# A two-block transformer step on one core: the two-sided matmul form also for the last merge gates and five output projections, and matmuls of one width in runs of eight

## What is computed

```python
u = jnp.einsum('bsd,de->bse', xn, w_in[l])
q, k, v, xr, gr, ga, gb = jnp.split(u, splits, axis=-1)
ya = chunked_band_attention(q, k, v, rel_table[l]) @ w_attn_out[l]
yb = (hr * jax.nn.gelu(gr)) @ w_rnn_out[l]
gates = jax.nn.sigmoid(jnp.concatenate([ga, gb], axis=-1) + b_merge[l])
h = h + (g_a * ya + g_b * yb) @ w_o[l]
gu = hn @ w_ffn_in[l]
h = h + (jax.nn.silu(g) * up) @ w_ffn_out[l]
...
    h = h + mix.astype(h.dtype)
    h = h + squared_relu_mlp(rmsnorm_2(h, mlp_norm_g[i]), mlp_w_up[i], mlp_w_down[i])
```

## Time and profile before

| | |
|---|---|
| median of 3 runs | 1126.56 us (1125.75 to 1126.63) |
| the profiled execution | 1126.75 us, its span 1125.0 us |
| PE busy, matmuls recorded | 1112.1 us (99%), 7954 |
| DVE, ACT, POOL busy | 765.5, 589.9, 218.3 us |
| mean granted clock of PE | 0.998 |

### The profile page before, as it was taken

One profiled execution on the slowest core, in us unless ns is written; L12 is line 12 of the kernel. 1 busy time (PEld: TensorE's weight loads), 2 busy tenths in 40 slices (PEclk: granted clock), 3 DMA queues, 4 the chain that ended last, 5 costly groups with the idle time before them and its releaser, 6 DMA issues.

```text
span 1125.0 us, 19980 instructions
## 1 busy us (share of the span) xinstructions
PE 1112.1 (99%) x7954; PEld 1037.1 (92%) x7954; DVE 765.5 (68%) x943; ACT 589.9 (52%) x791; POOL 218.3 (19%) x216
## 2 busy tenths in 40 slices
PE   8999999999999999999999999999999999999997
PEld 8999999999888889999999988888899999888887
DVE  6656985666877754699886777764467657876443
ACT  6547557535655543665664556643354445665332
POOL 2995003302000000167844010000030002000000
PEclk9999999999999999999999999999999999999999
DMA  9774442655655555446410356555545444655541
GB/s 296 214 229 150 150 140 93 224 181 175 200 186 186 186 192 188 145 149 188 150 39 2 112 164 197 195 192 186 187 150 188 151 145 148 198 191 214 188 149 38
DMA packets 154994, 187.31 MB, mean 166 GB/s; under 512 B 6544, under 2 KB 143920, under 8 KB 154928
## 3 DMA queue, kind: packets, MB, share of 16 engines
q1 hardware_dynamic: 151360, 184.06, 50.2%
q10 hardware_dynamic: 3568, 2.31, 0.7%
HBM read 185.29 MB, written 1.07 MB: 166 GB/s over the span
## 4 chain that ended last, share of the span: by engine, by line
PE 87%; POOL 5%; DVE 5%; issue 1%; ACT 1%; DMA 0%; DVEq 0%; SPq 0%; POOLq 0%; ACTq 0%
PE PS L445 18%; PE PS L492 12%; PE PS L386 10%; PE PS L387 9%; PE PS L388 9%; PE PS L447 9%; PE PS L494 6%; POOL XN L910 2%; DVE WL L382 2%; POOL XN L905 1%; POOL TAP L908 1%; PE PS L453 1%; PE PS L452 1%; PE PS L454 1%; PE PS L2012 1%; PE PS L2025 1%
## 5 line engine op out<-in xcount | busy, mean ns | idle before, releaser
L382 DVE TENSOR_TENSOR WL<-RAW,WH 128x2048 fp32r<-128x2048 f32 x170 | 399.5, 2352 | 213.1 <-ACT WH L373 213.0
L373 ACT ACTIVATE WH<-RAW 128x2048 fp32r<-128x2048 f32 x170 | 325.0, 1912 | 219.1 <-PE PS L494 121.1
L445 PE MATMUL PS<-XHL,WH 128*128 128x512 f32 x864 | 300.9, 395 | 0.0
L386 PE MATMUL PS<-XHL,WH 128*128 128x256 f32 x832 | 239.9, 288 | 3.6 <-DVE WL L333 2.4
L447 PE MATMUL PS<-XHL,WL 128*128 128x256 f32 x864 | 239.7, 277 | 0.0
L388 PE MATMUL PS<-XHL,WL 128*128 128x256 f32 x832 | 235.4, 283 | 0.0
L387 PE MATMUL PS<-XHL,WH 128*128 128x256 f32 x832 | 235.4, 283 | 0.0
L492 PE MATMUL PS<-HHL,WH 128*128 (+1 forms) x592 | 205.4, 394 | 0.0
L445 PEld LDWEIGHTS PS<-XHL,WH 128*128 128x128 f32 x864 | 162.1, 188 | 37.5
L386 PEld LDWEIGHTS PS<-XHL,WH 128*128 128x128 f32 x832 | 159.5, 192 | 7.2 <-issue 2.8
L494 PE MATMUL PS<-HHL,WL 128*128 (+1 forms) x592 | 164.0, 277 | 0.0
(11 more groups left out here) (310 smaller groups left out, 1669.7 us busy)
## 6 DMA issues: line engine op xcount, KB each, us to landing
RAW<-in_mlp_w_up SPq DMA_DIRECT2D x32, 1024.0 KB, 5.4
RAW<-in_mlp_w_down SPq DMA_DIRECT2D x32, 1024.0 KB, 5.0
RAW<-in_w_in SPq DMA_DIRECT2D x25, 1024.0 KB, 5.2
RAW<-in_w_ffn_in_pairs SPq DMA_DIRECT2D x22, 1024.0 KB, 5.1
RAW<-in_dn_w_in SPq DMA_DIRECT2D x16, 1024.0 KB, 5.8
RAW<-in_mb_w_in SPq DMA_DIRECT2D x12, 1024.0 KB, 5.1
RAW<-in_w_ffn_out SPq DMA_DIRECT2D x11, 1024.0 KB, 4.9
RAW<-in_w_attn_out SPq DMA_DIRECT2D x4, 1024.0 KB, 5.7
```

Of the source, the lines that this page charges most:

```text
L373: act.activation(WH[:, k], RAW[:, k], ACT.Copy).then_inc(hi_done, 1)
L382: dve.tensor_tensor(WL[:, k], RAW[:, k], WH[:, k].bitcast(F32), ALU.subtract).then_inc(lo_done, 1)
L386: pe.matmul(out, wh, xh, start=start, stop=False, skip_group_check=True)
L445: pe.matmul(out, h[:, k, part], XHL[:, k].rearrange("p e t -> p (e t)"), start=(k == 0), stop=False, skip_group_check=True)
```

## The change

The wide form is also used for the last four chunks of gab, for ao, ro (but its last chunk), wo, do and mo. `OH` and `OL` become halves of one tensor `OHL`, `DOH` and `DOL` of `DOHL`, so that 512 columns can be read in one matmul. A table `PAIRS` names the two banks of each such chunk. In every wide chunk the order of the matmuls changes: the 512-column ones of a block (or, in `multiply_rows`, of a k) come first, then its 256-column ones; in chunks in pieces, and where `multiply_rows` goes by b, in twos.

In gab, ao and ro ACT copies the second half to SBUF (`low_to`) and DVE adds the first (`add_to`), then multiplies as before. In wo, do and mo DVE adds both halves to `H`, one after the other. The last chunk of ro stays narrow (`halves_=False`) in the first half of its banks. The gate of the eighth chunk moves behind its copy.

```diff
+        PAIRS = {"qk": (4, 6, 2, 4, 6, 2, 4, 6), "gab": (None, None, None, None, 3, 5, 0, 3), "ao": (5, 0, 2, 4),
+                 "ro": (6, 0, 4, 2), "wo": (6, 4, 2, 6), "do": (6, 4, 2, 6), "mo": (5, 2, 0, 6)}
...
-            for n, (b, k) in enumerate(order_of(pieces)):
...
+            runs = [[(b, k) for k in range(KB)] for b in range(2)]
+            if pieces is not None:
+                runs = [[(b, k) for k in (p, p + 1)] for p in range(0, KB, 2) for b in range(2)]
+            for n, run in enumerate(runs):
...
-                pe.matmul(out, h[:, k, part], XHL[:, k].rearrange("p e t -> p (e t)"), start=(k == 0), stop=False,
-                          skip_group_check=True)
-                mm = pe.matmul(out[:, TOK:512], l[:, k, part], XH[:, k], start=False, stop=(k == KB - 1),
-                               skip_group_check=True)
+                for _, k in run:
+                    pe.matmul(out, h[:, k, part], both[:, k].rearrange("p e t -> p (e t)"), start=(k == 0), stop=False,
+                              skip_group_check=True)
+                for _, k in run:
+                    mm = pe.matmul(out[:, TOK:512], l[:, k, part], both[:, k, 0], start=False, stop=(k == KB - 1),
+                                   skip_group_check=True)
...
+            runs = [[(k, b) for b in range(KB)] for k in range(KROWS)]
+            if narrow or first or left == 3:
+                runs = [[(k, b) for k in range(KROWS)] for b in range(KB)]
...
+        def low_to(act, st, out):
+
+            act.wait_ge(mm_done, st.count())
+            act.activation(out, wide_sides(st)[1], ACT.Copy).then_inc(s_.part_out, 1)
+
+        def add_to(dve, st, out, n):
+
+            dve.wait_ge(s_.part_out, n)
+            return dve.tensor_tensor(out, out, wide_sides(st)[0], ALU.add)
...
                 merge_gate(2 * st.j - 8)
-                merge_gate(2 * st.j - 7)
+                if st.j < 7:
+                    merge_gate(2 * st.j - 7)
+                act.wait_ge(s_.scanned, 8)
+                low_to(act, st, GAB[:, 2 * st.j:2 * st.j + 2])
+            merge_gate(7)
...
                     dve.wait_ge(mm_done, st.count())
-                    dve.tensor_tensor(hb, hb, bank(st), ALU.add).then_inc(freed[st.slot], 1)
+                    ch(dve.tensor_tensor(hb, hb, wide_sides(st)[1], ALU.add))
+                    ch.wait(dve)
+                    dve.tensor_tensor(hb, hb, wide_sides(st)[0], ALU.add).then_inc(freed[st.slot], 1)
...
-            steps(pe, seg["ao"], lambda st: multiply(pe, st, OH, OL))
-            steps(pe, seg["ro"], lambda st: multiply(pe, st, XH, XL, (s_.y_done, 0) if st.j == 0 else None))
-            steps(pe, seg["wo"], lambda st: multiply(pe, st, OH, OL, (s_.ml_done, 0) if st.j == 0 else None))
+            steps(pe, seg["ao"], lambda st: multiply_wide(pe, st, both=OHL))
+            steps(pe, seg["ro"], lambda st: multiply_wide(pe, st, (s_.y_done, 0) if st.j == 0 else None, halves_=st.j < 3))
+            steps(pe, seg["wo"], lambda st: multiply_wide(pe, st, (s_.ml_done, 0) if st.j == 0 else None, both=OHL))
```

More of the change, by code:

```diff
@@ L430, in wide_sides, with multiply_wide @@
             return both[:, :, 0], both[:, :, 1]
-        def multiply_wide(pe, st, pieces=None, between=None):
+        def multiply_wide(pe, st, pieces=None, between=None, both=XHL, beside=None, halves_=True):
             pe.wait_ge(lo_done, st.count())
@@ L475, in multiply_rows @@
             first = st.i is None and st.j == 0
[L476 to L485, removed]
+            narrow = left in (1, 2)
@@ L486, in multiply_rows, with operands @@
+            def operands(k):
+                xhl = HHL[:, bass.ds(st.rel * KROWS + k, 1)].rearrange("p k e t -> p (k e t)")
+                return xhl, xhl[:, 0:TOK], xhl[:, TOK:512]
+            runs = [[(k, b) for b in range(KB)] for k in range(KROWS)]
+            if narrow or first or left == 3:
+                runs = [[(k, b) for k in range(KROWS)] for b in range(KB)]
+            for run in runs:
+                b = run[0][1]
+                if first and b % 2 == 0:
                     wide_bank_read(pe, wide, (2, 2, 6, 4)[b // 2])
-                if left == 2 and k == 0 and b % 2 == 0:
+                if left == 2 and b % 2 == 0:
@@ L488, in multiply_rows @@
                     pe.wait_ge(s_.low_added, 4 * (row_no[st.seg.name] - 1) + b // 2 + 1)
[L489 to L495, removed]
@@ L496, in multiply_rows @@
-                if left == 3 and b % 2 and k == KROWS - 1 and b < KB - 1:
+                for k, b in run:
+                    part = slice(b * P, b * P + P)
+                    xhl, xh, xl = operands(k)
+                    if narrow:
+                        mm = product(pe, PS[:, ROW_BANK[b], 0:TOK], h[:, k, part], l[:, k, part], xh, xl, False,
+                                     left == 1 and k == KROWS - 1)
+                    else:
+                        pe.matmul(PS[:, ROW_BANK[b]], h[:, k, part], xhl, start=first and k == 0, stop=False, skip_group_check=True)
@@ L497, in multiply_rows @@
+                for k, b in [] if narrow else run:
+                    mm = pe.matmul(PS[:, ROW_BANK[b], TOK:512], l[:, k, b * P:b * P + P], operands(k)[1], start=False,
+                                   stop=left == 3 and k == KROWS - 1, skip_group_check=True)
+                if left == 3 and b % 2 and b < KB - 1:
                     mm.then_inc(s_.low_rows, 1)
-                if left == 1 and b < KB - 1 and k == KROWS - 1 and (b % 2 or st.seg.name == "w1" and b == KB - 2):
+                if left == 1 and b < KB - 1 and (b % 2 or st.seg.name == "w1" and b == KB - 2):
@@ L1539, in _ @@
                     mix_lo(st.j - 1)
[L1540 to L1541 removed]
+                if st.j < 3:
+                    ch(add_to(dve, st, MU[:, blk], part_no("ro") + st.j + 1))
+                    ch.wait(dve)
+                    sum_ = MU[:, blk]
+                else:
+                    dve.wait_ge(mm_done, st.count())
+                    sum_ = wide_sides(st)[0]
+                dve.tensor_tensor(MU[:, blk], sum_, GAB[:, 8 + 2 * st.j:10 + 2 * st.j], ALU.mult).then_inc(freed[st.slot], 1)
                 dve.wait_ge(freed[st.slot], st.base // SLOTS + 1)
@@ L2150, in _ @@
             attn_pv(pe, 11)
-            steps(pe, seg["mo"], lambda st: multiply(pe, st, OH, OL, None if st.j else (s_.ol_done, 8)))
+            steps(pe, seg["mo"], lambda st: multiply_wide(pe, st, None if st.j else (s_.ol_done, 8), both=OHL))
             mlp(1)
```

48 lines of the change are left out of this document (33 added, 15 removed).

## The result

The changed kernel takes 1128.4 us (median of 17 runs, 1127.8 to 1129.3) where the kernel before takes 1126.5 beside it (17 runs, 1125.4 to 1127.0). The ratio is 1.0019, with a 95% interval of 1.0012 to 1.0026. The change makes the kernel slower by about 2 us; 1123.3 was forecast. The profiled execution of the changed kernel took 1128.9 us, its span 1127.2, against 1126.75 and 1125.0 before.

A forecast was written before the change was run, and what follows sets the result against it. PE, busy 99%, was taken as the bound: number of matmuls times their spacing. Terms -5.0 + 0.5 + 1.0 + 0.1 = -3.4 us, with 0 for the order, gave 1123.3 us; range 1102 to 1132.

The forecast's parts named there:

- The products that become wide: In 23 chunks of gates, attention and recurrence outputs, wo, do and mo, 368 products save 0.0137 us each: -5.0 us.
- The runs: Wide chunks in eights or twos: the new order moves no total, 0 us, with bounds of -18.9 and +8.3 us.
- reading by starts: Wide chunks in runs: 512 columns keep 0.2315 us, 256 pay 0.120; +8.3 us, 1131.5 us; chance 0.17.
- The cheaper runs: Wide chunks: a 512-column matmul behind its own kind falls to about 0.2155 us; 1104.6 us in all; chance 0.29.
- the skill's rule: Warm matmuls follow at N/2.4 + 2.5 ns, so 1824 wide products take 40 us less; kept as a rival.
- The gate wait: At the fifth gate chunk ACT's copy delays the eighth chunk's weight split, so PE waits: +0.5 us.
- The norm waits: After the last chunk of wo, do and mo, DVE's second addition makes PE wait 0.3 us, three times: +1.0 us.
- do: First do chunk: the saving in its first two pieces is lost, the third piece starting at about 628: +0.1 us.
- The slow start that goes: Before the norm sums 24 pairs take 0.354 us each instead of 0.347; whether that goes does not count.
- a pattern of its own: A long run of 512-column matmuls could have its own spacing pattern; named as a way to be wrong, without size.

The follow-up runs named there:

- experiment 5: Changed kernel with six blocks of 48 extra matmuls of various column and weight widths, onto a bank nothing reads, in one u0 chunk; 1174.5 us, single execution.
- experiment 2: Kernel before with only the matmul order changed, to runs of eight, in the chunks already wide; projections still narrow; 1129.5 us, ratio 1.0028.
- experiment 3: Changed kernel with runs of sixteen where possible, both blocks' 512-column matmuls before their 256-column ones; 1126.5 us, ratio 0.9999 to the kernel before.
- experiment 4: Changed kernel with runs of four instead of eight; 1131.3 us, ratio 1.0044 to the kernel before.
- experiment 1: Changed kernel with wide chunks in the old alternating order (512, 256, 512, 256) instead of runs; 1127.8 us, ratio 1.0012 to the kernel before.
- experiment 6: Changed kernel in alternating order, with the last chunk of wo, do and mo narrow; 1124.5 us, ratio 0.9985 to the kernel before.
- run 120: Not a follow-up run: "run" is a verb here, and 120 is the ns between starts of 256-column matmuls, 213 in some profiled executions.

## Why the prediction was wrong

**The products that become wide: right.** 368 matmuls fewer, and the projections gain. From the terms with the measured runs and waits one gets -5.0 + 0.9 (the runs in their own 23 chunks) + 0.5 + 1.6 + 0.1 - 0.5 (loose pairs that are gone, see below) = -2.4 us, against -2.3 in the three segments that hold nearly all of them.

**The runs: wrong, and this is the step that failed.** "Runs of either kind would move no total", so the term was 0. They moved it by +4.4 us, which turns -3.4 into +1.0. The prices of a settled matmul were read rightly, and experiment 5 gives them by themselves. What failed is the inference that the total of a mixed stream is their sum in whatever order. The kernel before showed only one order, and its alternation at 0.3467 happened to equal that sum. A run of eight has a settling stretch at its head that alternation in its dense pattern does not have; experiments 2, 3 and 4 show it by number of switches. The prediction's reading by starts was wrong in its numbers (0.2315 for every 512-column matmul of a run, against 0.2267 settled) yet right in its sign: measured are 5.587/16 = 0.3492 us a product, half-way between 0.3467 and 0.3515, and past the 1.9 ns from which it decides. It had 0.17.

**The cheaper runs and the skill's rule: wrong.** In their runs the 512-column matmuls settled at 0.227 us, not at 0.2155, and the plain f32 row said nothing about it. The Trainium skill (TensorE: Matmul & The Clock Gate, section "Back-to-back issue gap") gives N/2.4 + 2.5 ns, 216 for 512 columns and 109 for 256, as the gap of isolated matmuls, and about 131 ns for 512 columns in a stream of weight loads and matmuls. This case's trace has 227.3 and 119.8, and so agrees with the slope of the first, but not with its constant, and not with the 131. With weight loads of 128 new columns at each matmul and fp32r operands the constant here is 13.3.

**The gate wait: right.** Forecast 0.5 at about 195 us; the profile shows 0.23 at 195.79, and the start before it to this one is 505 ns, 385 more than the 120 of its neighbours, with another 0.11 to settle. It came by a second way too: DVE's multiplication of GAB took 1.42 us at 192.11, where the three others take 0.69 to 0.74.

**The norm waits: right in place and number, too small in size.** Three idle times of 0.26 us stand for the forecast 0.3, and the chain on POOL ends at 277.41 (274.75 + 2.66). But PE's loss by starts is 0.53 us each, so the term of 1.0 measures 1.6. (Its own slack, 0.73 - 0.46 three times, makes 0.8 and not 1.0.) The gate wait was counted by starts; these were sized by slack alone.

**do: right.** The wait on DOL is gone, PE idles 0.58 us for the norm rows instead and starts the third piece at 628.10 for the forecast 628.

**The slow start that goes: read past.** The prediction saw 24 pairs at 0.354 and set them aside because PE was held by POOL there. In the trace's nanoseconds these pairs have the spacings 233, 117, 241, 120, 236, 113: the loose pattern in plain sight, and the sign that one stream can have two totals. Against pairs at 0.347 they cost 0.17 us, three times 0.5, and in the change they are gone. The prediction named "a pattern of its own" as a way to be wrong and gave it no price.

**What is left.** -5.0 + 4.4 + 0.5 + 1.6 + 0.1 - 0.5 gives +1.1 us; the two spans differ by 2.2 and the medians by 2.0. Between the spans, 0.5 us is the start at the lower clock and 0.4 the longer end, both outside what the change touches, so 0.2 is left. How often either occurs in the executions that have no trace is not known, so the other 0.9 us between the medians stays open.

## What to carry to other kernels

Where PE is 99% busy, price a reordering of matmuls from a trace that shows that order, or give the switch its own unknown: a price per matmul is good only within the pattern from which it was read. If the same stream shows two spacings anywhere in a trace, even for 24 pairs, the second one can take a whole segment. Which one it takes can change between executions of the same instructions, so count matmuls in equal windows of each stage before a difference of two profiles is put down to an edit, and compare a stretch ahead of the edit first. And price a wait by the starts on both sides of it: 0.26 us of idle time were 0.53 us here.

## What the runs showed of the hardware

- A stream that alternates 512- and 256-column matmuls runs at 346.7 or at 353.3 ns a pair and keeps to it over more than 460 pairs. The same instructions fell into either (ao and ro in experiments 1 and 6). Why there are two, and what chooses, was not found.
- The return from 256- to 512-column matmuls costs about 28 ns spread over the next five, of which 7 come back at the 256-column ones.
- fp32r matmuls with 128 fresh weight columns follow at columns/2.4 GHz + 13.3 ns from 256 to 512 columns (119.8, 173.8, 227.3 with the first few unsettled ones), and at 110.6 for 128. With 64 weight columns they take 113.8 for 256 and 230 for 512, so the narrower load helped the short ones and hurt the long ones.
- At the start of the kernel the same 256-column matmuls run 120 or 213 ns apart, differently from one profiled execution to another: the 1001st matmul, ahead of every edit, starts between 128.64 us (experiment 1) and 131.54 us (experiment 3). In the changed kernel's profile the granted clock is 0.50 there, from 8.0 to 11.4 us.
